# The time steps' weight block second in the stream, and S5's small matmuls issued behind wide blocks of the projection

## The chip, the core and the metric

The kernel runs on one core of one Trainium2 chip. A core has five engines that each run their own program in order and meet only at semaphores: TensorE (PE, matmuls into eight PSUM banks), VectorE (DVE), ScalarE (ACT), GpSimd (POOL) and SyncE (SP, which here only issues DMAs). The metric is the device time of one execution in microseconds, less is better.

## What is computed

Two transformer-like blocks on 512 tokens of width 1024, in float32. The change touches the beginning of the first one, the projection of the normed input and what hangs on it:

```
h = rmsnorm(x, mix_norm_w)
proj = h @ w_in                                  # 1024 x 2828
y_s5 = s5_mixer(proj[:, :256], ...)              # u
y_ssd = ssd_mixer(z = proj[:, 256:1024], xbc = proj[:, 1024:2816], dt_raw = proj[:, 2816:2828], ...)
x = x + concat(y_s5, y_ssd) @ w_out
...
# s5_mixer: 16 groups of 16 channels, 64 complex states each
h_t = a * h_{t-1} + (b u_t);  y = Re(c h) + d u;  y = gelu(y) * sigmoid(gelu(y) @ w_glu)
# ssd_mixer: xbc = silu(causal_conv4(xbc)); dt = softplus(dt_raw + dt_bias); then chunked attention-like sums
```

After it come cross attention over a normed `mem` of 256 rows, a convolutional feed-forward layer, and a second block with two mixers and 16 routed experts.

## The kernel before

Activations lie with channels on partitions (128) and the 512 tokens along the free dimension. Every float32 product is made of three faster ones: a weight is split into a rounded high part `w_hi` and the rest `w_lo`, an activation into `hi` and `lo`, and `pe_fm` sums w_hi·hi, w_hi·lo and w_lo·hi over eight blocks of 128 input channels (lines 474 to 476). One output block of 128 channels is 24 matmuls of 128x512.

Weights come as a stream of slots in the order of the table `STREAM`; `slot_arrays` lays them out in DRAM in the same order. A slot is mostly 256 columns (two output blocks, 48 matmuls); `dt`'s is 128 columns (one block, 24 matmuls). For slot g: SP loads it into one of three raw buffers once DVE has finished slot g-3 (`sp_load`); ACT rounds it to `w_hi` (`act_split`, line 395) when the load is there and PE is through with slot g-2, which used the same of two buffers; DVE subtracts (`dve_split`, line 401); PE waits for DVE, and for the bank of four blocks ago to be emptied (`pe_block_start`). All of this is program order: `act_split_to(k, g)` and `dve_split_to(k, g)` stand where the author put them among the other work of ACT and DVE.

The projection's slots are u, three of xa, dt, xb, za, xc, zb, xd, zc, xe. `IN_TURNS` groups them in turns q = 0 to 4: (x0 x1 x2) (x3 z0) (x4 z1) (x5 z2) (x6), with x0 to x2 in xa and x3 to x6 in xb, xc, xd, xe; three functions walk over it, `pe_w_in`, `act_w_in` and `dve_w_in`. For each x block ACT copies the bank to `pad` and applies the first tap, DVE adds the other three (`dve_taps`), ACT applies silu, in order and one block behind; z blocks are one ACT instruction each.

S5's scan works on 128 chunks of 4 tokens with matrices made on the way:
- `dve_s5_powers` (powers `pw` of the eigenvalues), from which POOL builds the rotation tables `ec` and `es` (`pool_s5_tables`, `s5_double`), by doubling;
- `dve_s5_matrices` makes `bd`; `pe_s5_matrices` turns it by 16 transposes into banks 4 to 7; `act_s5_bt` copies them to `bt`;
- `dve_s5_outputs` makes `cb`; `pe_s5_lags` multiplies it with `bd`; `act_s5_lags` copies the result to `lags`;
- `act_s5_steps` copies `u` to `steps`, 16 copies of 32 partitions;
- for each half h: `pe_s5_in` (steps times bt, into banks 4 and 5), `dve_s5_step` (rotate, scan, rotate back), `pe_s5_out` (lags and cb, into bank 6 + h), `dve_s5_skip`.

Before the change the matrices, the block dt with its four transposes (`pe_dt`), the sum of squares of mem (`pe_norm_sum_all`, line 533) and the lags all stand between the third xa slot and xb, at the end of turn 0. `dve_s5_step` is a generator, issued in pieces between the taps of turns 1 and 2. Behind xe follow the keys (`pe_key`), which need the normed mem (`m_hi`, `m_lo`).

## Time and profile before

| | |
|---|---|
| median of 3 runs | 1543.58 us (1541.92 to 1544.74) |
| the profiled execution | 1542.16 us, span 1541.0 us |
| PE busy | 1420.1 us, 92% of the span |
| PEld (weight loads, beside PE) | 1162.2 us, 75% |
| DVE busy | 978.1 us, 63% |
| ACT busy | 753.3 us, 49% |
| POOL busy | 140.2 us, 9% |
| chain that ended last | PE 67%, DVE 8%, ACT 4%, issue 4%, DMA 1% |
| HBM | mean 150 GB/s over the span |

The page also cuts the span in 40 slices of 38.5 us. Each digit is the busy share in tenths; PEclk is TensorE's granted clock in tenths of full speed. The projection is in slices 1 to 6:

```
PE   7969979899989999999999998999999799999981
PEld 5758868778667888888888887886658688888861
DVE  4847557754325755456546558846545889889876
ACT  5374354544324322122324442245465788887863
PEclk9979999999999999999999999999999899999996
```

A busy PE means matmuls in flight, not matmuls at their peak; a wait is put down to what came last.

### The profile page before, as it was taken

What the parts mean: (1) busy time and instruction counts of PE and PEld (TensorE: products, weight loads), DVE (VectorE), ACT (ScalarE), POOL (GpSimd) and SP (SyncE); (2) the same over time, 40 slices, a digit from 0 to 9 for tenths busy, and PEclk for the clock granted to TensorE, in tenths of its full rate; (3) what the DMA queues carried; (4) which work ended last, traced back from release to release, by engine and by line L of the source; (5) the groups of instructions that cost most, each with busy time, mean ns of one, the idle gap of its engine ahead of it and who ended that gap; (6) DMA issues with size and microseconds to landing.
All of it is one profiled execution on the core that took longest, in us unless ns stands there. A gap on an engine that the chain in (4) does not pass through costs nothing.

```text
span 1541.0 us, 18286 instructions
## 1 busy us (share of the span) xinstructions
PE 1420.1 (92%) x7292; PEld 1162.2 (75%) x7292; DVE 978.1 (63%) x1321; ACT 753.3 (49%) x966; POOL 140.2 (9%) x165
## 2 busy tenths in 40 slices
PE   7969979899989999999999998999999799999981
PEld 5758868778667888888888887886658688888861
DVE  4847557754325755456546558846545889889876
ACT  5374354544324322122324442245465788887863
POOL 1600001100000000000000303200000111111012
PEclk9979999999999999999999999999999899999996
DMA  5112313312103342333123231110006799999975
GB/s 210 68 55 83 137 55 110 110 55 82 56 28 137 126 142 75 111 109 109 66 75 120 87 107 50 60 55 28 28 1 232 267 413 421 412 416 417 408 301 191
DMA packets 39332, 231.62 MB, mean 150 GB/s; under 512 B 4400, under 2 KB 5696, under 8 KB 17104
## 3 DMA queue, kind: packets, MB, share of 16 engines
q1 hardware_dynamic: 30640, 200.09, 34.5%
q0 software_dynamic: 7648, 27.87, 4.8%
q10 hardware_dynamic: 960, 2.49, 0.5%
q8 instruction: 58, 0.95, 0.2%
q14 instruction: 26, 0.21, 0.0%
HBM read 213.66 MB, written 16.78 MB: 150 GB/s over the span
## 4 chain that ended last, share of the span: by engine, by line
PE 67%; DVE 8%; ACT 4%; issue 4%; DMA 1%; POOL 0%; POOLq 0%; DVEq 0%; ACTq 0%
PE bank L474 13%; PE bank L476 12%; PE bank L475 12%; PE bank L3164 5%; PE bank L3166 5%; PE bank L3165 5%; PE bank L620 2%; DVE w_lo L401 1%; PE bank L493 1%; PE bank L494 1%; PE bank L495 1%; PE bank L2393 1%; PE bank L2414 1%; ACT w_hi L395 1%; PE bank L2159 1%
## 5 line engine op out<-in xcount | busy, mean ns | idle before, releaser
L474 PE MATMUL bank<-h_hi,w_hi 128*128 128x512 f32 x952 | 382.1, 401 | 14.1 <-DVE w_lo L401 11.1
L475 PE MATMUL bank<-h_lo,w_hi 128*128 128x512 f32 x952 | 372.2, 391 | 0.0
L476 PE MATMUL bank<-h_hi,w_lo 128*128 128x512 f32 x952 | 371.9, 391 | 0.0
L401 DVE TENSOR_TENSOR w_lo<-w_raw,w_hi 128x2048 fp32r<-128x2048 f32 (+3 forms) x86 | 188.5, 2192 | 116.7 <-ACT w_hi L395 116.1
L474 PEld LDWEIGHTS bank<-h_hi,w_hi 128*128 128x128 f32 x952 | 179.7, 189 | 59.8 <-DVE w_lo L401 14.4
L476 PEld LDWEIGHTS bank<-h_hi,w_lo 128*128 128x128 f32 x952 | 179.5, 189 | 38.2
L475 PEld LDWEIGHTS bank<-h_lo,w_hi 128*128 128x128 f32 x952 | 179.8, 189 | 37.2 <-issue 2.2
L395 ACT ACTIVATE w_hi<-w_raw 128x2048 fp32r<-128x2048 f32 (+3 forms) x87 | 154.8, 1779 | 61.8 <-PE bank L476 61.7
L3349 DVE TENSOR_TENSOR h_lo<-w_raw,h_hi 128x2048 fp32r<-128x2048 f32 x32 | 73.2, 2292 | 10.5 <-ACT h_hi L3250 8.7
L3349 DVE TENSOR_TENSOR lo_b<-raw_b,hi_b 128x2048 fp32r<-128x2048 f32 x32 | 73.2, 2290 | 7.0 <-ACT hi_b L3250 6.8
L474 PE MATMUL bank<-a_hi,w_hi 128*128 128x512 f32 x176 | 68.5, 389 | 0.0
L475 PE MATMUL bank<-a_lo,w_hi 128*128 128x512 f32 x176 | 68.5, 389 | 0.0
L476 PE MATMUL bank<-a_hi,w_lo 128*128 128x512 f32 x176 | 68.5, 389 | 0.0
L1795 ACT ACTIVATE gc<-gc 128x512 f32<-128x512 f32 x22 | 13.9, 632 | 111.4 <-DVE gc L1052 111.4
L3250 ACT ACTIVATE hi_b<-raw_b 128x2048 fp32r<-128x2048 f32 x32 | 61.5, 1921 | 5.7 <-PE bank L3166 5.6
L3250 ACT ACTIVATE h_hi<-w_raw 128x2048 fp32r<-128x2048 f32 x32 | 61.0, 1911 | 0.0
L3164 PE MATMUL bank<-h_hi,hh 128*128 128x512 f32 x128 | 51.2, 400 | 4.1 <-DVE hl L3379 2.6
L3164 PE MATMUL bank<-hi_b,xh 128*128 128x512 f32 x128 | 51.6, 403 | 1.5 <-DVE xl L3356 1.5
L3166 PE MATMUL bank<-lo_b,xh 128*128 128x512 f32 x128 | 50.2, 392 | 0.0
L3166 PE MATMUL bank<-h_lo,hh 128*128 128x512 f32 x128 | 50.1, 391 | 0.0
L3165 PE MATMUL bank<-h_hi,hl 128*128 128x512 f32 x128 | 50.1, 391 | 0.0
L3165 PE MATMUL bank<-hi_b,xl 128*128 128x512 f32 x128 | 49.9, 390 | 0.0
(610 smaller groups left out, 2748.9 us busy)
## 6 DMA issues: line engine op xcount, KB each, us to landing
w_raw<-in_params_dram SPq DMA_DIRECT2D x122, 1024.0 KB, 5.0
raw_b<-in_params_dram SPq DMA_DIRECT2D x51, 1024.0 KB, 8.1
w_raw<-in_params_dram SPq DMA_DIRECT2D x16, 704.0 KB, 4.0
result_rows<-osb POOLq DMA_DIRECT2D x16, 512.0 KB, 8.1
result_rows<-prm POOLq DMA_DIRECT2D x8, 512.0 KB, 3.2
xt<-in_x_t_dram POOLq DMA_DIRECT2D x1, 2048.0 KB, 12.5
scratch_rows<-htm SPq DMA_DIRECT2D x4, 512.0 KB, 2.9
out_dram<-pr SPq DMA_DIRECT2D x4, 512.0 KB, 2.6
```

The lines of the kernel that those rows point to most:

```text
L395: A.activation(k.w_hi[g % SPLIT][:, 0:size], k.raw[:, g % RAW, 0:size], ACT.Copy).then_inc(s.w_hi, 1)
L401: V.tensor_tensor(k.w_lo[g % SPLIT][:, 0:size], k.raw[:, g % RAW, 0:size], k.w_hi[g % SPLIT][:, 0:size].bitcast(F32), ALU.subtract).then_i ...
L474: PE.matmul(ps, wh, hi[:, c, 0:width], start=c == 0, stop=False)
L475: PE.matmul(ps, wh, lo[:, c, 0:width], start=False, stop=False)
L476: m = PE.matmul(ps, wl, hi[:, c, 0:width], start=False, stop=c == parts - 1)
L493: PE.matmul(ps, xh, wh, start=c == 0, stop=False)
L620: return k.nc.tensor.transpose(out, in_, k.ident[0:n, 0:n])
L3164: PE.matmul(o, xh[:, k0 + c, :], wh, start=first and c == 0, stop=False)
L3165: PE.matmul(o, xl[:, k0 + c, :], wh, start=False, stop=False)
L3166: m = PE.matmul(o, xh[:, k0 + c, :], wl, start=False, stop=final and c == 3)
L3250: done(A.activation(w_hi[n], raws[n], ACT.Copy), "w", n, c)
L3349: done(V.tensor_tensor(w_lo[n], raws[n], w_hi[n].bitcast(F32), ALU.subtract), "w", n, c)
```

## The change

`dt` becomes the second slot of the stream, behind u, and its block is multiplied there; its ACT copy goes to `xbc` block 11 (before 13), and its four transposes follow the first xa slot. S5's transposes of bd follow xb (x3); the lags, and then the sum of squares of mem, follow za (z0); `pe_s5_in(0)` follows xc, `pe_s5_in(1)` and `pe_s5_out(0)` follow xd, `pe_s5_out(1)` follows xe. ACT and DVE issue their parts at matching places: ACT's copies of bt behind x3, of lags and the root of mem's norm behind z0; DVE's `dve_s5_outputs` between the split behind x3 and x3's taps, each `dve_s5_step` in one piece at the end of turns 2 and 3. The table `es` moves from `sz` to `xbc` blocks 12 and 13, so ACT's wait for the last rotation moves from z2 to x block 12. The diff:

```diff
--- before.py
+++ after.py
@@ -93,7 +93,7 @@
 
 
 
-STREAM = [("u", 1, "aa"), ("xa", 3, "aa"), ("dt", 1, "a"), ("xb", 1, "aa"), ("za", 1, "aa"), ("xc", 1, "aa"), ("zb", 1, "aa"),
+STREAM = [("u", 1, "aa"), ("dt", 1, "a"), ("xa", 3, "aa"), ("xb", 1, "aa"), ("za", 1, "aa"), ("xc", 1, "aa"), ("zb", 1, "aa"),
           ("xd", 1, "aa"), ("zc", 1, "aa"), ("xe", 1, "aa"),
           ("wk", 4, "aa"), ("wv", 4, "aa"), ("w_out", 4, "vv"), ("wq", 4, "aa"), ("wo", 4, "vv"),
           ("up0", HB, "vv"), ("dn0", DB, "v"), ("up1", HB, "vv"), ("dn1", DB, "v"),
@@ -148,7 +148,7 @@
 def slot_arrays(a):
 
     xbc, z = columns(a["w_in"][0], 1024, 1792), columns(a["w_in"][0], 256, 768)
-    s = columns(a["w_in"][0], 0, 256) + xbc[:3] + columns(a["w_in"][0], 2828 - P, P, P)
+    s = columns(a["w_in"][0], 0, 256) + columns(a["w_in"][0], 2828 - P, P, P) + xbc[:3]
     s += [xbc[3], z[0], xbc[4], z[1], xbc[5], z[2], xbc[6]]
     for n in ("xa_wk", "xa_wv", "w_out", "xa_wq", "xa_wo"):
         s += columns(a[n][0], 0, D)
@@ -243,7 +243,7 @@
         self.pad = m("pad", [P, 2, T + 3])
         self.tt = self.sz[:, 0:4, :].rearrange("p a t -> p (a t)").rearrange("p (i j l) -> p i j l", i=2, j=8)
         self.rm = self.rs[:, 0:MEM]
-        self.ec, self.es = m("ec", [P, TILES, CHUNKS]), self.sz[:, 4:6, :].rearrange("p a (t c) -> p (a t) c", c=CHUNKS)
+        self.ec, self.es = m("ec", [P, TILES, CHUNKS]), self.xbc[:, 12:14, :].rearrange("p a (t c) -> p (a t) c", c=CHUNKS)
         x = Memory(nc, x_at, h_at)
         self.bu, self.gg = x("bu", [P, 2, TILES // 2, CHUNKS]), x("gg", [P, 2, TILES // 2, CHUNKS])
         self.steps, self.lags = x("steps", [P, TILES, CHUNKS]), x("lags", [P, TILES, P])
@@ -976,17 +976,14 @@
     v(V.tensor_tensor(t0, im, es, ALU.mult))
     v(V.tensor_tensor(g1, im, ec, ALU.mult))
     v(V.tensor_tensor(t1, re, es, ALU.mult))
-    yield
     v.own()
     v(V.tensor_tensor(g0, g0, t0, ALU.add))
     v(V.tensor_tensor(g1, g1, t1, ALU.subtract))
-    yield
     v.own()
     for t in range(4):
         mag = k.mag[:, STEPS - 1, 4 * h + t:4 * h + t + 1].broadcast_to([P, CHUNKS])
         for part, g in enumerate((g0, g1)):
             v(V.tensor_tensor_scan(bu[part][:, t, :], mag, g[:, t, :], 0.0, ALU.mult, ALU.add))
-    yield
     v.own()
     V.tensor_tensor(g0, bu[0], ec, ALU.mult).then_inc(s.s5_rot, 1)
     V.scalar_tensor_tensor(g1, bu[1], -1.0, es, ALU.mult, ALU.mult).then_inc(s.s5_rot, 1)
@@ -1082,23 +1079,28 @@
     for c in range(DB):
         for j in range(2):
             pe_fm(k, "u", 0, j, k.hi, k.lo, "mix", first=c, stop=c + 1)
+    pe_fm(k, "dt", 0, 0, k.hi, k.lo, cols=P)
     for q, turn in enumerate(IN_TURNS):
         for x, (part, n) in enumerate(turn):
             stage, slot = in_slot(part, n)
             for j in range(2):
                 pe_fm(k, stage, slot, j, k.hi, k.lo)
-            if x == 0 and q in (2, 3):
-                pe_s5_out(k, q - 2)
-            if x == 0 and q in (1, 2):
-                pe_s5_in(k, q - 1)
-        if q == 0:
-            PE.wait_ge(s.n_rs, 1)
-            pe_s5_matrices(k)
-            pe_fm(k, "dt", 0, 0, k.hi, k.lo, cols=P)
-            PE.wait_ge(s.s5_bt, 4)
-            pe_norm_sum_all(k, "mem", k.msq, MEM, 7)
-            pe_dt(k)
-            pe_s5_lags(k)
+            if (part, n) == ("x", 0):
+                PE.wait_ge(s.n_rs, 1)
+                pe_dt(k)
+            elif (part, n) == ("x", 3):
+                pe_s5_matrices(k)
+            elif (part, n) == ("z", 0):
+                PE.wait_ge(s.s5_bt, 4)
+                pe_s5_lags(k)
+                pe_norm_sum_all(k, "mem", k.msq, MEM, 7)
+            elif (part, n) == ("x", 4):
+                pe_s5_in(k, 0)
+            elif (part, n) == ("x", 5):
+                pe_s5_in(k, 1)
+                pe_s5_out(k, 0)
+            elif (part, n) == ("x", 6):
+                pe_s5_out(k, 1)
     for b in range(2):
         pe_key(k, b)
     pe_ssd_sums(k)
@@ -1112,7 +1114,7 @@
     PE, s = k.nc.tensor, k.s
     PE.wait_ge(s.evac_a, EMPTIED[BLOCK0["dt"]][1])
     for t in range(TT):
-        m = pe_turn(k, k.bank[4][:, t * P:t * P + P], k.xbc[:, XBC_B - 1, t * P:t * P + P])
+        m = pe_turn(k, k.bank[4][:, t * P:t * P + P], k.xbc[:, 11, t * P:t * P + P])
     m.then_inc(s.dt_turn, 1)
 
 
@@ -1130,8 +1132,10 @@
         act_norm_hi(k, "mix", k.sq0, k.hi, 0, b, T)
     act_split_to(k, 1)
     act_s5_angle(k)
+    act_split_to(k, SLOT0["xa"])
     for j in range(2):
         act_empty(k, BLOCK0["u"] + j, k.u[:, j, :])
+    act_empty(k, BLOCK0["dt"], k.xbc[:, 11, :])
 
     def silu(blk):
         A.wait_ge(s.conv, blk + 1)
@@ -1149,6 +1153,8 @@
                         A.wait_ge(s.pads_zero, 1)
                     if blk >= 2:
                         A.wait_ge(s.conv, blk - 1)
+                    if blk == 12:
+                        A.wait_ge(s.s5_rot, 8)
                     act_empty(k, i, k.pad[:, blk % 2, 3:T + 3])
                     A.wait_ge(s.evac_a, EMPTIED[i][1])
                     A.activation(k.xbc[:, blk, :], k.pad[:, blk % 2, 0:T], ACT.Identity, bias=k.col("ssd_cb", blk),
@@ -1158,8 +1164,6 @@
                 else:
                     if n == 0 and j == 0:
                         A.wait_ge(s.s5_tab, 2)
-                    elif n == 2 and j == 0:
-                        A.wait_ge(s.s5_rot, 8)
                     act_empty(k, i, k.sz[:, 2 * n + j, :], ACT.Silu)
             if part == "x" and n == 6:
                 silu(XBC_B - 1)
@@ -1173,12 +1177,11 @@
                 A.wait_ge(s.mem, 16)
                 for b in range(DB):
                     act_square(k, "mem", k.mt, k.msq, b, MEM)
-        if q == 0:
-            act_s5_bt(k)
-            act_split_to(k, SLOT0["dt"] + 1)
-            act_empty(k, BLOCK0["dt"], k.xbc[:, XBC_B - 1, :])
+            if (part, n) == ("x", 3):
+                act_s5_bt(k)
+        if q == 1:
+            act_s5_lags(k)
             act_norm_root(k, "mem", k.rm, k.bank[7][:, 0:MEM], D)
-            act_s5_lags(k)
             act_ssd_steps(k)
 
 
@@ -1189,13 +1192,15 @@
     dve_norm_split(k, "mix", k.xt, k.col("mix_norm", 0, DB), k.sq0, k.rs, k.hi, k.lo, 0, DB, T, slot=0)
     dve_split_to(k, 1)
     dve_s5_powers(k)
+    dve_split_to(k, SLOT0["xa"])
     for q, turn in enumerate(IN_TURNS):
-        step = dve_s5_step(k, q - 1) if q in (1, 2) else iter(())
         for n_, (part, n) in enumerate(turn):
             stage, slot = in_slot(part, n)
             dve_split_to(k, SLOT0[stage] + slot + 1)
-            if q == 0 and n_ == 1:
+            if (part, n) == ("x", 1):
                 dve_s5_matrices(k)
+            elif (part, n) == ("x", 3):
+                dve_s5_outputs(k)
             if part == "x":
                 for j in range(2):
                     blk = 2 * n + j
@@ -1204,19 +1209,16 @@
             if part == "x" and n == 6:
                 dve_norm_split(k, "mem", k.mt, k.col("mem_norm", 0, DB), k.msq, k.rm, k.mhi, k.mlo, 0, DB, MEM)
                 dve_split_to(k, SLOT0["wk"] + 1)
-            for _ in range(3):
-                next(step, None)
-        for _ in step:
-            pass
-        if q == 0:
-            dve_split_to(k, SLOT0["dt"] + 1)
-            dve_s5_outputs(k)
-            V.wait_ge(s.dt_turn, 1)
-            tm = k.bank[4][:, :].rearrange("p (t c) -> p t c", t=TT)[:, :, P - SSD_H:P]
-            V.tensor_copy(k.dtr[:, :, :], tm).then_inc(s.dt_out, 1)
+            if (part, n) == ("x", 0):
+                V.wait_ge(s.dt_turn, 1)
+                tm = k.bank[4][:, :].rearrange("p (t c) -> p t c", t=TT)[:, :, P - SSD_H:P]
+                V.tensor_copy(k.dtr[:, :, :], tm).then_inc(s.dt_out, 1)
+        if q == 1:
             dve_ssd_steps(k)
-        if q in (2, 3):
-            dve_s5_skip(k, q - 2)
+        elif q in (2, 3):
+            dve_s5_step(k, q - 2)
+        if q in (3, 4):
+            dve_s5_skip(k, q - 3)
```

What this does to the order of instructions, at three places. First ACT, behind its second split; w_hi_53 and w_hi_54 are the two buffers of the high part, u, xbc and pad what is copied from PSUM (+ is the kernel after):

```order
-L395 ACTIVATE w_hi_54<-w_raw 128x2048
+L395 ACTIVATE w_hi_54<-w_raw 128x1024
 L685 ACT_TABLE_LOAD
 L685 ACTIVATE s5sc<-s5sc 128x8
 L686 ACTIVATE s5sc<-s5sc 128x8
+L395 ACTIVATE w_hi_53<-w_raw 128x2048
 L504 ACTIVATE u<-bank 128x512 x2
-L395 ACTIVATE w_hi_53<-w_raw 128x2048
```

The second split is dt's half slot, and xa's first split stands ahead of the copies of u instead of behind them.

DVE, behind the powers pw; w_lo_55 and w_lo_56 are the two buffers of the low part. Before:

```order
L731 TENSOR_TENSOR pw<-s5sc 128x8
L401 TENSOR_TENSOR w_lo_55<-w_raw,w_hi_53 128x2048
L1052 SCALAR_TENSOR_TENSOR xbc<-pad,prm,xbc 128x512 x6
L401 TENSOR_TENSOR w_lo_56<-w_raw,w_hi_54 128x2048
L745 TENSOR_TENSOR lam<-pw,mag 128x2x8 x3
L746 TENSOR_TENSOR s5t<-pw 128x16
L747 TENSOR_TENSOR s5t<-pw 128x16
L749 TENSOR_TENSOR lam<-s5t 128x8
```

and after:

```order
L731 TENSOR_TENSOR pw<-s5sc 128x8
L401 TENSOR_TENSOR w_lo_55<-w_raw,w_hi_53 128x2048
L401 TENSOR_TENSOR w_lo_56<-w_raw,w_hi_54 128x2048
L1049 SCALAR_TENSOR_TENSOR xbc<-pad,prm,xbc 128x512 x6
L1215 COPY dtr<-bank 128x48
L401 TENSOR_TENSOR w_lo_55<-w_raw,w_hi_53 128x2048
L745 TENSOR_TENSOR lam<-pw,mag 128x2x8 x3
L746 TENSOR_TENSOR s5t<-pw 128x16
```

The split behind the powers was that of xa's second slot and is now that of its first, which PE takes next; another whole split follows ahead of the first taps, and the copy of the time steps (dtr) stands ahead of the split in front of the matrices (lam).

PE, around the small matmuls (bd transposed, msq summed, xbc transposed for dt, cb times bd). Before:

```order
L476 MATMUL bank3<-h_hi_58,w_lo1_56 128x512
L620 MATMUL bank4<-ident_62,bd_89 128x128 x4
L620 MATMUL bank5<-ident_62,bd_89 128x128 x4
L620 MATMUL bank6<-ident_62,bd_89 128x128 x4
L620 MATMUL bank7<-ident_62,bd_89 128x128 x4
...
L476 MATMUL bank0<-h_hi_58,w_lo0_55 128x512
L533 MATMUL bank7<-msq_104,ones_63 128x256 x8
L620 MATMUL bank4<-ident_62,xbc_68 128x128 x4
L882 MATMUL bank5<-cb_78,bd_89 32x128 x8
L882 MATMUL bank6<-cb_78,bd_89 32x128 x8
L474 MATMUL bank1<-h_hi_58,w_hi1_54 128x512
```

and after:

```order
L476 MATMUL bank2<-h_hi_58,w_lo1_56 128x512
L620 MATMUL bank4<-ident_62,bd_89 128x128 x4
L620 MATMUL bank5<-ident_62,bd_89 128x128 x4
L620 MATMUL bank6<-ident_62,bd_89 128x128 x4
L620 MATMUL bank7<-ident_62,bd_89 128x128 x4
L474 MATMUL bank3<-h_hi_58,w_hi0_53 128x512
...
L476 MATMUL bank0<-h_hi_58,w_lo0_55 128x512
L882 MATMUL bank5<-cb_78,bd_89 32x128 x8
L882 MATMUL bank6<-cb_78,bd_89 32x128 x8
L533 MATMUL bank7<-msq_104,ones_63 128x256 x8
L474 MATMUL bank1<-h_hi_58,w_hi1_54 128x512
```

The 16 transposes have 48 wide matmuls of xb ahead of them and za's behind; lags and sum have changed places and stand behind za; dt's block (bank0 above) and its transposes are gone from here.

## Rows read from the trace of the kernel before

**Rows 1.** Instructions in order of time on PE: start, length (us), engine, line, what, [idle before].

```profile
37.25 0.50 PE L474 MATMUL bank<-h_hi,w_hi 128*128 128x512 f32 x1 [0.16 <-DVE w_lo L401]
...
70.19 0.39 PE L476 MATMUL bank<-h_hi,w_lo 128*128 128x512 f32 x1
...
73.48 3.05 PE L620 MATMUL bank<-ident,bd 128*128 128x128 f32 x16 [2.90 <-DVE bd L799]
...
84.01 0.80 PE L474 MATMUL bank<-h_hi,w_hi 128*128 128x512 f32 x1 [7.49 <-DVE w_lo L401]
...
94.62 5.17 PE L533 MATMUL bank<-msq,ones 128*128 128x256 f32 x15 [3.12 <-ACT bt L838]
...
104.84 5.34 PE L882 MATMUL bank<-cb,bd 128*32 128x128 f32 x32 [4.40 <-DVE cb L826]
...
110.11 0.50 PE L474 MATMUL bank<-h_hi,w_hi 128*128 128x512 f32 x1
```

**Rows 2.** Stretches: length, busy PE, PEld, DVE, ACT, POOL, then PEclk, DMA.

```profile
37.20:110.10 72.90, 54.91 (x236) 44.40 (x236) 47.80 (x115) 39.74 (x60) 24.91 (x42) 0.86 0.19 66
110.10:199.70 89.60, 89.59 (x689) 74.90 (x688) 52.27 (x74) 36.50 (x46) 2.95 (x4) 1.00 0.31 106
73.40:76.50 3.10, 3.02 (x16) 2.68 (x16) 2.99 (x5) 0.78 (x2) 0.00 (x0) 0.62 0.00 0
84.00:91.50 7.50, 7.49 (x24) 5.72 (x24) 4.42 (x6) 6.75 (x12) 0.00 (x0) 0.75 0.40 140
94.60:99.80 5.20, 5.18 (x16) 4.28 (x17) 3.26 (x3) 3.67 (x3) 0.00 (x0) 0.67 0.00 0
104.80:110.10 5.30, 5.26 (x32) 4.49 (x32) 0.60 (x3) 1.50 (x4) 0.00 (x0) 0.68 0.01 3
173.10:177.70 4.60, 4.60 (x162) 4.34 (x161) 2.82 (x4) 3.73 (x4) 0.00 (x0) 1.00 0.02 4
```

**Rows 3.** Order of time on ACT, around the first copies to steps.

```profile
75.72 0.63 ACT L1138 ACTIVATE xbc<-xbc 128x512 f32<-128x512 f32 x1 [14.85 <-DVE xbc L1052]
...
76.26 5.36 ACT L850 ACTIVATE steps<-u 32x256 f32<-32x256 f32 x8
...
81.64 1.06 ACT L395 ACTIVATE w_hi<-w_raw 128x1024 fp32r<-128x1024 f32 x1
```

**Rows 4.** Order of time on DVE, S5's matrices and the split behind them.

```profile
59.23 2.04 DVE L745 TENSOR_TENSOR lam<-pw,mag 128x16 f32<-128x16 f32 x3
...
64.87 0.15 DVE L753 TENSOR_TENSOR s5sc<-s5sc 128x8 f32<-128x8 f32 x1
...
73.36 4.56 DVE L1052 SCALAR_TENSOR_TENSOR xbc<-pad,prm,xbc 128x512 f32<-128x512 f32 x6
...
82.73 1.23 DVE L401 TENSOR_TENSOR w_lo<-w_raw,w_hi 128x1024 fp32r<-128x1024 f32 x1 [4.80 <-ACT w_hi L395]
```

**Rows 5.** Order of time on POOL, the last instruction of the tables.

```profile
63.62 1.29 POOL L899 TENSOR_TENSOR sz<-sz 128x512 f32<-128x512 f32 x1
```

**Rows 6.** Order of time on ACT, behind the second split.

```profile
34.89 1.28 ACT L685 ACT_TABLE_LOAD   x1
...
36.30 0.19 ACT L686 ACTIVATE s5sc<-s5sc 128x8 f32<-128x8 f32 x1
```

**Rows 7.** Order of time on DVE, the powers and the split behind them.

```profile
37.11 0.16 DVE L719 TENSOR_TENSOR s5sc<-s5sc 128x8 f32<-128x8 f32 x1
...
42.96 2.29 DVE L401 TENSOR_TENSOR w_lo<-w_raw,w_hi 128x2048 fp32r<-128x2048 f32 x1
```

**Rows 8.** Order of time on ACT, the norm of mem to the time steps.

```profile
101.83 0.42 ACT L542 ACTIVATE rs<-rs 128x256 f32<-128x256 f32 x1
...
108.53 3.58 ACT L862 ACTIVATE lags<-bank 32x128 f32<-32x128 f32 x8 [6.28 <-PE bank L882]
...
115.67 1.90 ACT L395 ACTIVATE w_hi<-w_raw 128x2048 fp32r<-128x2048 f32 x1
```

**Rows 9.** Order of time on PE, the first matmul of the keys.

```profile
205.17 0.55 PE L474 MATMUL bank<-m_hi,w_hi 128*128 128x256 f32 x1 [5.48 <-DVE m_lo L554]
```

## The prediction

> **What bounds the kernel now.** I read the page first: PE is busy 92% of the span, DVE 63%, ACT 49%, and the chain that ended last is mostly matmuls. So the end is set by TensorE's program order plus the places where TensorE stands still, and a change that moves nothing but order can only win or lose such places. Next, the busy time by stretch [rows 2]. The change touches the input projection. Its second part, 110.1 to 199.7 us, is full: 89.59 of 89.60 us busy at granted clock 1.00, so the other engines are always early enough there. The first part, 37.2 to 110.1 us, is not: 54.91 of 72.90 us busy, clock 0.86. Then the instructions of PE in order of time [rows 1], for the idle time in the brackets. Three 256-column slots (u is done by 37.1) run through without a pause until 70.6. Behind them PE waits 2.90 us for DVE's bd, does 16 transposes, waits 7.49 us for the dt slot's low part, multiplies dt, waits 3.12 us for ACT's copies of bt, sums the squares of mem, waits 4.40 us for DVE's cb, and does the lags. That is 17.9 us of waiting. It is a row of small steps, each with an answer from DVE or ACT, and no wide block of matmuls stands between them to cover the answer.
>
> The clock makes it dearer. In the four small pieces it was granted at 0.62, 0.75, 0.67 and 0.68 [rows 2], that is partly at 1.2 and partly at 2.4 GHz, after waits of 2.9 to 7.5 us; in the full stretches it is 1.00. At 1.00 the pieces would take 1.9, 5.6, 3.5 and 3.6 us for 3.1, 7.5, 5.2 and 5.3: 6.5 us lost.
>
> **What the change does to these pieces.** The dt slot (24 matmuls) goes to second place, so its split stands ahead of xa's. The transposes of bd follow xb instead of the third xa slot; the lags and the sum of mem follow za; s5's inputs follow xc and xd, its outputs follow xd and xe. TensorE's instructions are the same ones; nothing is added. If every answer comes during the 11 us of a wide slot, the ledger is: 17.9 us of waits gone, 6.5 us of slow clock gone, and a third term: the second output block (4.6 us at clock 1.00) [rows 2] now stands behind xe. There PE waits 5.48 us for the normed mem in any case [rows 9], a chain of ACT and DVE that starts at xe's end, so the 4.6 us are hidden and some 0.9 us of that wait stays. Credit: 17.9 + 6.5 + 4.6 = 29.0 us.
>
> **What is late instead: xa's first split.** Two debits stand against that, and I work them out from times of DVE and ACT. The slot unit first: 144 matmuls from 37.25 to 70.19 [rows 1], so 0.23 us each, 11.0 us a wide slot, 5.5 us for dt. PE leaves u at 37.1 and dt at 42.6. xa's first slot uses u's buffers of the high and low part, so ACT splits it only after u, at 37.1 to 39.0, and DVE takes it after its powers (they stand ahead of it in its program). The powers take 42.96 - 37.11 = 5.85 us [rows 7]. They begin when ACT's table load and two sines are over: 36.49 - 34.89 = 1.6 us behind its split [rows 6], and this split is now of half a slot, 1.06 us for 1.90 [rows 3, 8], so it ends at 34.05. Powers then 35.65 to 41.5, split 2.29 us [rows 7], done 43.8. PE starts xa at 43.85: a wait of 1.2 us, and everything in xa comes 6.6 us later than now. A wait as short as this costs no clock, I take; in the worst case it costs what followed the 2.9 us wait, 1.2 us.
>
> **What is late instead: xb's split.** This is the large debit. The 7.49 us wait was not the transposes' fault. DVE starts S5's matrices at 59.23 behind the third xa split, reaches the taps at 73.36 [rows 4], and ACT, in order, holds its silu for those taps 14.85 us; then come 5.36 us of copies to steps, and only then the next split [rows 3]. The change leaves these where they are. The split behind them is now xb's, a whole slot, and dt's short slot with its transposes no longer stands there. Chain: the matrices start at 59.23 + 6.6 = 65.8. Of their 14.1 us, the nine small instructions up to 64.87 took 5.6 us, three of them 2.04 us, where the like instruction after it took 0.15 us [rows 4]. POOL's tables end at 64.9 [rows 5]; they start from the powers, 1.5 us earlier now (35.65 for 37.11), so they end near 63.5 and are clear of the matrices. I price the nine at 1.3 us, hence 1.3 + 8.5 = 9.8 us: done 75.6. Taps to silu 2.36, silu to steps 0.54, steps to split 5.38 [rows 3, 4]: 83.9. Split to matmul was 84.01 - 81.64 = 2.37 for half a slot; a whole one adds 0.84 on ACT and 1.06 on DVE (2.29 for 1.23) [rows 4, 7]: 4.3, so xb starts at 88.1. PE comes out of xa at 70.6 + 6.6 and 0.5 for dt's four transposes, 77.7. It waits 10.4 us. Behind it, as behind the 7.49 us wait, the slow clock: 7.5 - 5.6 = 1.9 us.
>
> The Trainium skill, SBUF — State Buffer, section Who interferes with whom, says that a DVE instruction with two SBUF inputs and a GpSimd instruction that reads SBUF exclude each other for a whole instruction, each in turn. By that rule the 4.3 us of relief are real, as soon as POOL is through; without it, the nine might be slow by themselves (broadcast operands), and the relief would be nothing. This case's rows lean to the rule: the fast 0.15 us begins at 64.87, the moment at which POOL ends.
>
> **Is anything late behind xb?** From 88.1: xb with slow clock to 101.0, transposes 1.9, za to 113.9, lags 3.6, mem's sum 3.5, so xc from 121.0 to 132.0. The tightest is zb's split, since ACT does the root of mem's norm, then the time steps, ahead of it: root done 102.25 - 99.8 = 2.4 us behind the sum, then 115.67 - 112.1 = 3.6 [rows 8], splits 1.9 + 2.3: 131.3. PE needs it after xc and s5's first input, at 1.7 us ((89.6 - 7 x 11.0 - 2 x 4.6) / 2) [rows 2]: 133.7. Slack 2.4 us. bt's copies follow the taps of block 6, which stand behind cb (about 6 us of DVE): some 111 against 113.9. DVE's scans (9 us) now run in one piece, 138 to 147, against 155 when PE asks; x block 12 waits for the second scans, done some 12 us before. SP loads in the new order, each slot's load is let go three slots ahead, as now. POOL's reload of xt (2 MB) waits for the second output block and moves with it, far ahead of its use. All at nothing; each would show as a wait of PE.
>
> **Sum.** Credit 29.0; debits 1.2 + 10.4 + 1.9 = 13.5; and 0.1 for rounding: 15.4 us. The profiled execution took 1542.16 us (span 1541.0, 1.2 around it): 1526.8. The median of the runs is 1.4 higher, so 1528.2. Ends for the uncertain terms: relief 0 instead of 4.3; small wait's clock 1.2; lags, sum and transposes as long as today (4.6 in all) if the clock dips again; the other way, no slow clock behind the wait, 1.9, and xa's third split earlier by what POOL is out of its way, some 0.7. One by one and added up: 1525.6 to 1538.3.
>
> **Rivals.** A, the matrices stay slow: the nine instructions take 5.6 us wherever they stand, or POOL is slower in its new company and runs into them. Then xb starts at 92.4, 11.1 us are gained: 1532.5. For it: POOL has to share DVE with a split and taps meanwhile, as today. Against: the 64.87 boundary. 15%.
> B, a second wait behind xb: zb's slack of 2.4 us is used up, and ACT's queue, with lags, roots and time steps in one row, passes its lateness on to DVE's splits, each of which starts the next. One missed slot costs up to a wide slot, 11 us, once more: 1539, up to no gain. For it: ACT and DVE are in order and share one chain. Against: the stretch from 110 us is full today under nearly this load. 6%.
> C, the other side: the clock. The new 10.4 us wait is the longest of the stage. If TensorE stayed at 1.2 GHz not for part of a slot but through xb, the transposes, za, the lags and mem's sum (31 us of work), it would lose 31 us instead of 1.9, and the kernel would be 13.7 us slower: 1557.3. It decides from 17 us of work at the low level on. Against: after 7.49 us of waiting the clock was back within the 24 matmuls of dt (0.75 on the mean). 3%. The Trainium skill, TensorE: Matmul & The Clock Gate, section Seeing it yourself, tells of a clock seen stuck low over a long stretch; no row here shows it.
> D, that the change does nothing: the waits come back somewhere else in full, as the keys need mem's norm anyway. The chain there starts at xe's end, and xe's end is what moves. 3%.
>
> **Chances.** My forecast 73%, A 15%, B 6%, C 3%, D 3%. The range of 1524 to 1536 holds the forecast's and A's ends with the 1.4 us between runs; outside are the most of B, C and D. This kernel's measurement tells 0.2%, 3.1 us, from no change. Faster by more: 0.93; within: 0.03; slower: 0.04.
>
> **What would show it.** Right: PE's idle time between 37 and 185 us is two waits, about 1.2 us ahead of xa and about 10 ahead of xb, the second released by DVE's split of xb, with ACT's silu still held for DVE's taps; clock 1.00 in lags and mem's sum; the small instructions of the matrices at 0.15 us; the keys start near 189.8 instead of 205.17, after 1 us of waiting; and behind it the same trace, shifted. Wrong: a wait above 13 us at xb (A), any wait at zb, xd or zc (B), a clock below 1.00 behind za (C). Should the keys start at 190 and the end move by less, the loss is in later stages, which I take as shifted as a whole.

## The result: 1.0% faster, where the forecast was 1.0%

The changed kernel took 1527.51 us (median of four, 1525.25 to 1528.59), the kernel before beside it 1543.28 (1541.92 to 1544.74): a ratio of 0.9896, with a 95% interval of 0.9879 to 0.9913. The forecast was 1528.2 us. A second set of five runs of the same changed kernel, told below, gave 1527.16. Two executions of 3667 us, one of the kernel before in a later set and one of the kernel with the second output block in its old place, are left out of all medians here.

The profiled execution took 1525.25 us, with a span of 1524.1 for the 1541.0 of before. It is the fastest of the nine executions of this kernel in the two sets; the second trace, told below, is of the slowest, 1531.33 us. TensorE is busy 1413.3 us (93%), DVE 975.3, ACT 752.5, GpSimd 140.6. The first view to read is again TensorE's order of time. Columns as in [rows 1]: start, length, engine, line, what, and in brackets the idle time before it.

```profile
43.80 0.50 PE L474 MATMUL bank<-h_hi,w_hi 128*128 128x512 f32 x1 [1.70 <-DVE w_lo L401]
...
87.02 0.80 PE L474 MATMUL bank<-h_hi,w_hi 128*128 128x512 f32 x1 [9.79 <-DVE w_lo L401]
...
99.57 1.91 PE L620 MATMUL bank<-ident,bd 128*128 128x128 f32 x16
...
112.30 3.68 PE L882 MATMUL bank<-cb,bd 128*32 128x128 f32 x32
115.91 3.72 PE L533 MATMUL bank<-msq,ones 128*128 128x256 f32 x16
...
130.38 1.95 PE L934 MATMUL bank<-steps,bt 128*128 128x128 f32 x16
...
187.87 0.36 PE L474 MATMUL bank<-m_hi,w_hi 128*128 128x256 f32 x1 [0.99 <-DVE m_lo L554]
...
190.78 0.39 PE L474 MATMUL bank<-m_hi,w_hi 128*128 128x256 f32 x1 [0.93 <-DVE m_lo L554]
...
208.44 1.98 PE L1023 MATMUL bank<-u,wglu 128*128 128x512 f32 x4 [0.99 <-ACT u L1003]
```

Against [rows 1]: the waits ahead of the transposes (2.90), of the sum of mem (3.12) and of the lags (4.40) are gone; these three pieces carry no bracket at all. The wait ahead of a slot's low part is still there, 7.49 us before and 9.79 now, but a wide slot, xb's, stands behind it. The other new wait is ahead of xa. Its bracket shows 1.70 us, but a bracket only measures from the last matmul that was recorded, and in other executions of this kernel and its variants the same gap is shown as 0.23 to 1.74 with xa starting at 43.3 to 44.1 in all eleven; so the start is the number to read. The keys begin at 187.87 for 205.17 [rows 9].

The stretches of the same trace (length, busy PE, PEld, DVE, ACT, POOL, then granted clock, DMA):

```profile
36.00:111.50 75.50, 64.02 (x284) 52.47 (x284) 51.40 (x118) 42.86 (x61) 24.49 (x42) 0.93 0.25 84
87.00:100.00 13.00, 12.98 (x52) 10.66 (x53) 7.01 (x8) 10.60 (x15) 0.00 (x0) 0.87 0.23 81
99.50:101.50 2.00, 2.00 (x18) 1.93 (x17) 1.97 (x5) 1.42 (x2) 0.00 (x0) 1.00 0.49 78
112.30:115.90 3.60, 3.60 (x33) 3.41 (x32) 2.60 (x3) 2.46 (x7) 0.00 (x0) 1.00 0.25 34
115.90:119.60 3.70, 3.70 (x18) 3.27 (x18) 0.00 (x0) 3.19 (x6) 0.00 (x0) 1.00 0.60 250
110.00:186.00 76.00, 76.00 (x627) 64.67 (x629) 47.58 (x72) 37.87 (x51) 0.00 (x0) 1.00 0.25 84
```

These answer to [rows 2]. The transposes, the lags and the sum of mem had 0.62, 0.68 and 0.67; each now follows a wide slot and runs at 1.00. The lags take 3.6 us for 5.3. What is left of the slow clock sits in xb, 0.87, behind the long wait. From 110 to 186 us TensorE is busy without a gap, so nothing is late behind xb.

The chain that sets xb's start, on ACT, answering to [rows 3]:

```profile
76.82 0.63 ACT L1142 ACTIVATE xbc<-xbc 128x512 f32<-128x512 f32 x1 [8.92 <-DVE xbc L1049]
77.36 5.35 ACT L850 ACTIVATE steps<-u 32x256 f32<-32x256 f32 x8
82.73 1.91 ACT L395 ACTIVATE w_hi<-w_raw 128x2048 fp32r<-128x2048 f32 x1
```

and on DVE, answering to [rows 4] and [rows 7]:

```profile
41.45 2.29 DVE L401 TENSOR_TENSOR w_lo<-w_raw,w_hi 128x2048 fp32r<-128x2048 f32 x1
...
65.06 0.33 DVE L745 TENSOR_TENSOR lam<-pw,mag 128x16 f32<-128x16 f32 x3
...
65.96 0.16 DVE L753 TENSOR_TENSOR s5sc<-s5sc 128x8 f32<-128x8 f32 x1
...
74.46 4.56 DVE L1049 SCALAR_TENSOR_TENSOR xbc<-pad,prm,xbc 128x512 f32<-128x512 f32 x6
84.67 2.29 DVE L401 TENSOR_TENSOR w_lo<-w_raw,w_hi 128x2048 fp32r<-128x2048 f32 x1 [5.65 <-ACT w_hi L395]
...
127.23 2.29 DVE L401 TENSOR_TENSOR w_lo<-w_raw,w_hi 128x2048 fp32r<-128x2048 f32 x1 [1.52 <-ACT w_hi L395]
```

The eight small instructions of S5's matrices ahead of L753 run from 65.06 to 65.96, 0.90 us for 5.64 before; three of them are 0.33 us for 2.04. (The prediction and the expectations count them as nine; the traces have eight up to L753's start.) ACT's silu still waits for DVE's taps, 8.92 us for 14.85. Then silu, copies to steps, split, split, xb: the same chain as before, link for link. GpSimd's last table instruction, answering to [rows 5]:

```profile
61.70 1.28 POOL L899 TENSOR_TENSOR xbc<-xbc,sz 128x512 f32<-128x512 f32 x1
```

It ends at 62.98, ahead of the matrices at 65.06. Before, it ended at 64.91, and they had begun at 59.23.

### The profile page after: what moved, and what is told of

The parts are those of the page before. It is cut to its first block, busy times and chain, and to the rows that moved or that the text cites. A ratio compares the mean times of both kernels' runs of the same rounds, so it can differ in the third digit from the quotient of the medians.

```text
span 1524.1 us, 18285 instructions
## 1 busy us (share of the span) xinstructions
PE 1413.3 (93%) x7292; PEld 1157.5 (76%) x7292; DVE 975.3 (64%) x1321; ACT 752.5 (49%) x966; POOL 140.6 (9%) x165
## 4 chain that ended last, share of the span: by engine, by line
PE 67%; DVE 8%; ACT 4%; issue 4%; DMA 1%; POOL 0%; POOLq 0%; DVEq 0%; ACTq 0%
PE bank L474 13%; PE bank L476 12%; PE bank L475 12%; PE bank L3166 5%; PE bank L3168 5%; PE bank L3167 5%; PE bank L620 2%; DVE w_lo L401 2%; PE bank L493 1%; PE bank L495 1%; PE bank L494 1%; PE bank L2416 1%; PE bank L2395 1%; ACT w_hi L395 1%; PE bank L2161 1%
## 5 line engine op out<-in xcount | busy, mean ns | idle before, releaser
L474 PE MATMUL bank<-h_hi,w_hi 128*128 128x512 f32 x952 | 381.2, 400 | 17.9 <-DVE w_lo L401 14.9
L401 DVE TENSOR_TENSOR w_lo<-w_raw,w_hi 128x2048 fp32r<-128x2048 f32 (+2 forms) x86 | 187.8, 2184 | 107.1 <-ACT w_hi L395 106.5
L395 ACT ACTIVATE w_hi<-w_raw 128x2048 fp32r<-128x2048 f32 (+2 forms) x87 | 154.8, 1780 | 62.9 <-PE bank L476 62.9
L1797 ACT ACTIVATE gc<-gc 128x512 f32<-128x512 f32 x22 | 13.9, 632 | 111.4 <-DVE gc L1049 111.4
```

Source lines behind the costliest of these rows:

```text
L395: A.activation(k.w_hi[g % SPLIT][:, 0:size], k.raw[:, g % RAW, 0:size], ACT.Copy).then_inc(s.w_hi, 1)
L401: V.tensor_tensor(k.w_lo[g % SPLIT][:, 0:size], k.raw[:, g % RAW, 0:size], k.w_hi[g % SPLIT][:, 0:size].bitcast(F32), ALU.subtract).then_i ...
L474: PE.matmul(ps, wh, hi[:, c, 0:width], start=c == 0, stop=False)
```

## Experiments

The theory that is tested is the prediction's ledger: each wait saved or added is worth its length and the slow clock behind it; the wait ahead of xb is DVE's and ACT's chain behind S5's matrices. Each experiment has its own rival, in its expectation. All diffs are against the changed kernel, save for the first one. "The changed kernel" is put at 1527.3 us, the median of its nine runs in two sets. The gated block is S5's last step, u times wglu, and its start on TensorE (L1023, after ACT's 0.99 us) is the mark by which the traces are compared behind the keys.

### The dt block alone

The kernel before, with nothing but the dt slot in second place: its splits ahead of xa's, TensorE's dt matmuls and transposes behind the third x slot. All S5 work stays where it was.

```diff
-STREAM = [("u", 1, "aa"), ("xa", 3, "aa"), ("dt", 1, "a"), ...
+STREAM = [("u", 1, "aa"), ("dt", 1, "a"), ("xa", 3, "aa"), ...
...
             pe_s5_matrices(k)
-            pe_fm(k, "dt", 0, 0, k.hi, k.lo, cols=P)
```

> The kernel before with dt's slot second in the stream, its block behind u and its transposes behind the first xa slot; the transposes of bd, mem's sum and the lags stay between xa and xb, the outputs where they were. Ledger theory (the gain is waits taken away plus clock, part by part): xa ends at 77.1, the transposes follow at once, then PE waits for bt until about 97 (ACT does both groups of copies to steps first), sum and lags 9 us, xb starts near 106 for 110.1 before. About 4 us faster than before: 1539.5. Rival (dt's place carries the gain, the rest moves what was hidden): all of the change's 15.8 us, 1527.5.

Measured: 1538.01 us, ratio to the kernel before 0.997 (0.9956 to 0.9983). TensorE in order of time:

```profile
76.77 1.91 PE L620 MATMUL bank<-ident,bd 128*128 128x128 f32 x16
97.33 6.72 PE L533 MATMUL bank<-msq,ones 128*128 128x256 f32 x16 [18.65 <-ACT bt L838]
```

A wait of 18.65 us stands behind the transposes, in front of the sum of mem, because bt's copies on ACT stand behind the taps, steps and a split. The waits of 2.90, 7.49, 3.12 and 4.40 have become this one, and behind it the sum of mem runs at the low clock (6.72 us for the 3.72 in the changed kernel). The keys start at 202.67, after 5.48 us as before. The ledger's 1539.5 stands against the rival's 1527.5: by the medians dt's place alone is worth 4 us of the 16 (2.5 us at the keys' start and 2.8 at the gated block in this one trace), and the rest comes from the S5 pieces moving behind wide slots.

### The early splits

xb's and za's splits are taken out of the queue behind the taps: ACT splits xb ahead of the silus of blocks 2 and later, DVE directly behind S5's matrices; the steps, bt's copies and za's split move up in the same way.

```diff
+                    if blk == 3:
+                        act_split_to(k, SLOT0["xb"])
+                        act_s5_steps(k, (0, 1))
+                    elif blk == 5:
+                        act_split_to(k, SLOT0["za"])
+                    elif blk == 7:
+                        act_s5_bt(k)
...
                 dve_s5_matrices(k)
+                dve_split_to(k, SLOT0["xb"])
...
+                    if blk == 5:
+                        dve_split_to(k, SLOT0["za"])
```

> The changed kernel with xb's split taken out from behind the silu that waits for DVE: ACT splits xb behind x block 3's first tap and does the first half of the copies to steps there, DVE takes it behind the matrices, ahead of the taps; za's split likewise behind x block 5's first tap; ACT's copies of bt ahead of the silu of block 6. Ledger theory: xb's low part is there at 76.7, xa ends at 77.1, so the 9.8 us wait and 1.5 us of slow clock go and no other wait takes their place: 11.3 us faster than the changed kernel, 1516.2. Rival (ACT and DVE are one full chain, and the wait only moves on to za or zb): under 3 us faster, 1525 or more.

Measured: 1513.74 us, ratio 0.9817 (0.9797 to 0.9836).

```profile
43.86 0.50 PE L474 MATMUL bank<-h_hi,w_hi 128*128 128x512 f32 x1 [0.37 <-DVE w_lo L401]
...
88.02 1.91 PE L620 MATMUL bank<-ident,bd 128*128 128x128 f32 x16
...
176.35 0.36 PE L474 MATMUL bank<-m_hi,w_hi 128*128 128x256 f32 x1 [1.00 <-DVE m_lo L554]
...
197.34 1.98 PE L1023 MATMUL bank<-u,wglu 128*128 128x512 f32 x4 [0.99 <-ACT u L1003]
```

No bracket between 43.86 and 176.35: the wait ahead of xb is gone, and no other took its place. The transposes start 11.55 us earlier (88.02 for 99.57), which is the wait of 9.79 and the slow clock of xb behind it. That is the ledger's price for this wait. It reaches the end: 11.1 us at the gated block (197.34 for 208.44), and 13.6 us by this median, 10.4 by that of a second set of runs, told below.

### Does GpSimd slow the small instructions?

The theory of the 4.3 us term: the eight small instructions are slow only while GpSimd's tables run. Test: xa's first split ahead of DVE's powers, which removes the wait ahead of xa but starts the tables 6.5 us later, so that they run into the matrices again.

```diff
-    dve_s5_powers(k)
     dve_split_to(k, SLOT0["xa"])
+    dve_s5_powers(k)
```

> The changed kernel with DVE's split of xa's first slot ahead of the powers, not behind. PE's 1.7 us wait ahead of xa goes. If DVE's small instructions were slow because of POOL: the powers, and with them POOL's tables, come 5.4 us later, the tables end near 68 and lie over the nine small instructions of the matrices, which take about 5.6 us for 0.9: xb starts 2.6 us or more later, 1530. Rival (POOL plays no part): 1.7 us faster, 1525.8.

Measured: 1532.54 us, ratio 0.9936 (0.9917 to 0.9956), so slower than the changed kernel by 5 us. On DVE:

```profile
64.25 2.04 DVE L745 TENSOR_TENSOR lam<-pw,mag 128x16 f32<-128x16 f32 x3
...
69.88 0.15 DVE L753 TENSOR_TENSOR s5sc<-s5sc 128x8 f32<-128x8 f32 x1
```

on GpSimd:

```profile
62.13 3.09 POOL L894 TENSOR_TENSOR sz<-xbc,pw 128x512 f32<-128x512 f32 x1
...
68.65 1.27 POOL L899 TENSOR_TENSOR xbc<-xbc,sz 128x512 f32<-128x512 f32 x1
```

and on TensorE:

```profile
90.95 0.80 PE L474 MATMUL bank<-h_hi,w_hi 128*128 128x512 f32 x1 [14.54 <-DVE w_lo L401]
```

The same three instructions take 2.04 us again, and they are fast from 69.88 on; GpSimd's last table instruction ends at 69.92. Before, the pair of times was 64.87 and 64.91. In both kernels the boundary follows GpSimd and not the place in the program. GpSimd pays too: one 128x512 instruction that takes 1.05 us in the changed kernel took 3.09 here, beside DVE's split, as it did in the kernel before. xb starts at 90.95 for 87.02. I had expected 3 us of loss and measured 5: behind the wait of 14.54 us xb takes 13.5 us for 12.6, and the keys' part is 0.5 us longer.

The ends show how: GpSimd's instructions in this trace end at 66.26, 67.29, 68.68 and 69.92 us, and DVE's long instructions at 66.29, 67.31, 68.71 and 69.96, each 0.02 to 0.04 us behind one of GpSimd's; the two between them take 0.16 and 0.17 us. The Trainium skill (SBUF — State Buffer, section Who interferes with whom) says that a DVE instruction with two SBUF inputs contends with a GpSimd instruction that reads SBUF, for ports that only one of them holds at a time. The trace agrees: 5.63 us here against 0.90 in the changed kernel for the same eight instructions.

### The second output block in its old place

```diff
-            elif (part, n) == ("x", 6):
+            elif (part, n) == ("z", 2):
                 pe_s5_out(k, 1)
```

> The changed kernel with the second output block behind zc, ahead of xe, and not behind xe. Ledger theory: its 4.6 us come back onto the path, since the chain of mem's norm starts at xe's end; PE's wait ahead of the keys grows from 1.0 to 5.5 us; 4.5 us slower than the changed kernel, 1532.0. Rival (the keys' wait is set elsewhere): no difference, 1527.5.

Measured: 1528.16 us (median of five), ratio 0.9907 (0.9889 to 0.9926): 0.9 us slower than the changed kernel, where 4.5 were expected. The intervals overlap, so the medians alone would not show that it is slower at all.

```profile
193.06 0.55 PE L474 MATMUL bank<-m_hi,w_hi 128*128 128x256 f32 x1 [5.47 <-DVE m_lo L554]
...
211.66 1.98 PE L1023 MATMUL bank<-u,wglu 128*128 128x512 f32 x4 [0.99 <-ACT u L1003]
```

The wait ahead of the keys is back at 5.47 us, as expected, and the keys start 4.4 to 5.2 us later than in the two traces of the changed kernel (187.87 and 188.63). But the gated block starts only 2.2 to 3.2 us later: from the keys' start to it, this kernel takes 18.60 us, and the changed one 20.57. So part of the hidden block's worth is lost between keys and gated block. In the changed kernel's trace, DVE there:

```profile
189.11 0.85 DVE L562 SCALAR_TENSOR_TENSOR msq<-mt,prm,rs 128x256 f32<-128x256 f32 x1
189.88 0.85 DVE L554 TENSOR_TENSOR m_lo<-msq,m_hi 128x256 fp32r<-128x256 f32 x1
```

and GpSimd:

```profile
188.98 1.48 POOL L604 TENSOR_SCALAR_AFFINE_SELECT afm<-afm 128x512 fp32r<-128x512 f32 x2
```

GpSimd waits for the second output block before it reloads xt and builds afm. Both moved with the block, and the two selects now meet DVE's norm of mem: two instructions take 0.85 us each for 0.48 and 0.42. (The memset just ahead of the selects, 188.37 to 188.91 us, slows nothing: DVE's two instructions beside it take 0.48 and 0.41.) TensorE waits a second time (0.93 us at 190.78 above), and behind that wait its clock dips:

```profile
193.50:196.50 3.00, 3.00 (x18) 3.00 (x17) 0.00 (x1) 2.99 (x3) 0.00 (x0) 0.56 0.63 254
```

### GpSimd's work behind mem's norm

```diff
+    G.wait_ge(s.m_mul, DB)
     k.g(G.memset(exact, -1.0))
...
-    G.wait_ge(s.m_mul, DB)
```

> The changed kernel, with GpSimd's memset and two affine selects of afm held until DVE has normed the last block of mem. Theory (GpSimd's selects slow two of DVE's instructions of mem's norm from 0.48 and 0.42 to 0.85 us, the keys wait a second time for m_lo, and their matmuls run at a lower clock behind that wait): DVE's L562 and L554 all at 0.4 to 0.5 us, one wait of 1.0 us ahead of the keys and no second one, keys to gated block 18.6 us for 20.6 to 20.9, so glu starts about 206.5. Time 2 us under the changed kernel's 1527.3: 1525.3. Rival 1 (the selects only stand where DVE would be slow anyway): keys to glu stays 20.6 to 20.9 and the time 1527.3. Rival 2 (the pieces behind it take the gain back, since the clock after each later wait varies from run to run by as much): glu 2 us earlier, time 1527.3.

Measured: 1524.78 us, ratio 0.9886 (0.9868 to 0.9903). TensorE:

```profile
187.80 0.36 PE L474 MATMUL bank<-m_hi,w_hi 128*128 128x256 f32 x1 [1.00 <-DVE m_lo L554]
...
206.40 1.98 PE L1023 MATMUL bank<-u,wglu 128*128 128x512 f32 x4 [0.99 <-ACT u L1003]
```

and DVE:

```profile
189.03 0.48 DVE L562 SCALAR_TENSOR_TENSOR msq<-mt,prm,rs 128x256 f32<-128x256 f32 x1
189.43 0.42 DVE L554 TENSOR_TENSOR m_lo<-msq,m_hi 128x256 fp32r<-128x256 f32 x1
```

Keys to gated block is 18.60 us again, with one wait; the two instructions are back at 0.48 and 0.42. The first theory holds in the trace to a tenth: 2.0 us earlier at the gated block. The medians say 2.5 us, which agrees but would not prove it, as the intervals overlap.

Of the 2.0 us, the two instructions explain 0.8. The rest is about the price of the clock, 0.56 in the stretch above and 1.00 in this kernel: from 193.36 to 195.93 us twelve matmuls of the changed kernel start 0.21 us apart, where they start 0.12 apart here, an estimate of 1.1 us. A low clock does not cost the same everywhere: with the output block in its old place the keys begin at 0.50 (193.0 to 196.0 us), are back at 1.00 from 198.8, and their stretch still takes 9.90 us, as here at 1.00 throughout (9.91). There the dip falls on the first keys, which have to wait for DVE's m_lo at either clock; in the changed kernel it comes when DVE is done and TensorE sets the pace. No run parts the wait from the clock behind it.

### TensorE kept at work in the wait

80 transposes of the identity into a bank that nobody reads, ahead of xb.

```diff
+            if (part, n) == ("x", 3):
+                pe_keep_on(k, 6, 80)
             for j in range(2):
                 pe_fm(k, stage, slot, j, k.hi, k.lo)
```

> The changed kernel with 80 more transposes of the identity into bank 6, which nobody reads, in PE's 9.8 us wait ahead of xb (80 x 0.119 = 9.5 us); they compute nothing. If the wait costs its length and, behind it, the slow clock: xb takes 11.0 us for 12.55, 1.5 us faster than the changed kernel. Rival (the clock behind the wait is not tied to PE standing still): no difference.

Measured: 1523.45 us, ratio 0.9888 (0.9868 to 0.9908).

```profile
76.86 8.90 PE L620 MATMUL bank<-ident 128*128 128x128 f32 x80
87.09 0.50 PE L474 MATMUL bank<-h_hi,w_hi 128*128 128x512 f32 x1 [1.33 <-DVE w_lo L401]
...
98.12 1.91 PE L620 MATMUL bank<-ident,bd 128*128 128x128 f32 x16
```

xb starts at the same time (87.09 for 87.02) and takes 11.03 us for 12.55. So against the first trace the slow clock behind the wait costs 1.5 us, and the gated block starts at 206.92, again 1.5 us earlier. By the medians it is 3.8 us. The two ratios to the kernel before, 0.9896 and 0.9888, are not told apart by their intervals, so the 1.5 us of the trace is the figure to keep.

### The transposes of bd in the wait

The same place, but with useful work: the 16 transposes go ahead of xb instead of behind it.

```diff
+            if (part, n) == ("x", 3):
+                pe_s5_matrices(k)
             for j in range(2):
                 pe_fm(k, stage, slot, j, k.hi, k.lo)
...
-            elif (part, n) == ("x", 3):
-                pe_s5_matrices(k)
```

> The changed kernel with the 16 transposes of bd in the wait ahead of xb and not behind xb; bd is there at 74.4, xa ends at 77.1. Ledger theory: a small piece put into a wait costs nothing, behind a wide block it costs its length: 1.9 us faster than the changed kernel, the slow clock in xb as before. Rival (what stands behind a wide block is free): no difference.

Measured: 1524.76 us, ratio 0.9881 (0.986 to 0.9902).

```profile
77.10 1.91 PE L620 MATMUL bank<-ident,bd 128*128 128x128 f32 x16
87.09 0.79 PE L474 MATMUL bank<-h_hi,w_hi 128*128 128x512 f32 x1 [8.08 <-DVE w_lo L401]
```

The transposes fit into the wait, which is 8.08 us instead of 9.79, and xb starts at the same time. The lags start at 110.78 and the keys at 186.36, both 1.5 us earlier than in the first trace of the changed kernel and 2.3 earlier than in the second, whose xb was slower; that brackets the 1.9 us expected. The gated block starts at 206.11, 2.3 us earlier than in the first trace, as the keys' stretch was shorter too. So behind xb the transposes cost their length, and in the wait they cost nothing. Ahead of xb in the kernel before they had a wait of 2.90 us in front of them and ran at 0.62; neither is there now, as bd is done before xa ends.

### The changed kernel once more

> The changed kernel once more, unaltered, beside the others on one chip, as what they are compared with: 1526 to 1528 by every theory.

Measured: 1527.16 us, ratio 0.9898 (0.988 to 0.9916).

```profile
87.07 0.80 PE L474 MATMUL bank<-h_hi,w_hi 128*128 128x512 f32 x1 [9.79 <-DVE w_lo L401]
...
100.29 1.91 PE L620 MATMUL bank<-ident,bd 128*128 128x128 f32 x16
```

xa starts at 43.86 and xb at 87.07, behind the same 9.79 us, but the transposes at 100.29 instead of 99.57. So xb took 13.2 us here and 12.55 in the first trace, by the same program: the slow clock behind the same wait cost 2.3 and 1.7 us, over the 10.9 us of a slot at full clock (xc, from the end of mem's sum at 119.5 to the first input at 130.4).

### The best version, twice

The early splits together with GpSimd's work behind mem's norm (both diffs above).

> The kernel with the early splits (e4) and POOL's memset and two selects on afm held back until DVE has normed mem. In the changed kernel these fall on DVE's norm of mem, one pair of its instructions takes 0.85 us each for 0.48 and 0.42. If POOL is the reason: 0.8 us faster than e4, some 1513. Rival: no difference from e4, 1513.7.

Measured: 1512.93 us, ratio 0.9802 (0.9782 to 0.9821). This is the fastest so far, but only 0.8 us ahead of the early splits' 1513.74, and not the 2.6 us that its own trace shows at the gated block (194.73 for 197.34). At 418 us the two traces stand at the same transposes again (418.49 and 418.74). To see whether that is the program or chance, both ran again side by side.

> The early splits once more, beside the next kernel on one chip. By both theories the median lies at 1513 to 1515 us, keys at 176.3 and glu at 197.3 us in the trace. If the clock behind the later waits is a matter of chance, the time at which the time-step scans' last matmuls run (275 to 287 us, granted clock 0.89 in the first run of this kernel, 0.77 in that of the next) has another clock this time.

> The early splits with GpSimd's afm work behind mem's norm, once more, beside the kernel without the latter on one chip. If the 2.6 us that it is ahead at the gated block reach the end, its median is 2 to 2.6 us under the other's: 1511 to 1512. If the slow clock behind the later waits takes them back, the medians are equal within 1 us. In the trace: keys at 176.1, glu at 194.7, and the piece from 272 to 286 us at a granted clock of 0.77 again if the arrival time decides it, at another clock if chance does.

Measured, early splits: 1516.86 us, ratio 0.9836 (0.982 to 0.9853). With GpSimd's work later: 1512.43, ratio 0.9819 (0.9801 to 0.9837). One piece of the program shows a part of what the trace of the later version had lost. It begins behind a wait of 3.2 us on DVE, with the last products of the scan over chunks (the piece that the expectations name by its 275 to 287 us), and ends where the next norm is multiplied. Stretches as above: length, busy PE, PEld, DVE, ACT, POOL, granted clock, DMA. Early splits, the keys' stretch and this piece in the first set, then the piece in the second:

```profile
176.30:188.60 12.30, 11.16 (x64) 10.53 (x64) 8.48 (x15) 7.94 (x12) 2.69 (x5) 0.72 0.53 175
...
275.00:287.10 12.10, 10.84 (x63) 8.51 (x63) 7.52 (x12) 6.41 (x8) 0.00 (x0) 0.89 0.00 1
```
```profile
274.20:285.80 11.60, 9.45 (x62) 7.17 (x62) 7.40 (x12) 6.41 (x8) 0.00 (x0) 1.00 0.01 1
```

With GpSimd's work later, first and second:

```profile
176.10:186.00 9.90, 9.26 (x64) 7.91 (x64) 6.43 (x14) 7.96 (x12) 2.61 (x5) 1.00 0.63 214
...
272.30:285.60 13.30, 11.99 (x62) 9.53 (x62) 7.54 (x13) 6.41 (x8) 0.00 (x0) 0.77 0.00 1
```
```profile
272.10:283.70 11.60, 9.46 (x62) 7.17 (x62) 7.41 (x12) 6.41 (x8) 0.00 (x0) 1.00 0.01 1
```

In the keys' stretch the later version is ahead: 9.9 us at a clock of 1.00 for 12.3 at 0.72 (in the second set 9.9 for 11.4 at 0.85). In the other piece, the busy time of DVE and ACT is the same in all four (7.4 to 7.5 and 6.4 us); the granted clock is 0.89, 1.00, 0.77 and 1.00, and the piece lasts 12.1, 11.6, 13.3 and 11.6 us. One program has had both the slowest and the fastest of them. So the clock behind such a wait is not fixed by the program, and this piece alone moves an execution by 1.7 us. In the first set it took 1.1 us of the lead. Most of the rest went in the last 14 us ahead of the transposes at 418: from 404.80 they took 13.9 us at a clock of 0.88, and 12.3 at 1.00 in the early splits' trace. Over both sets of ten runs the version with GpSimd's work later has a median of 1512.7 us and the early splits 1514.8: 2.1 us, beside the 2.6 and 2.1 us that the two pairs of traces show at the gated block (194.73 for 197.34, 194.48 for 196.60). The runs of the two kernels overlap.

## Why the prediction was right

The median, 1527.5, lies 0.7 us under the forecast. Step by step, with the times at which TensorE starts each piece:

```
                       forecast   first trace   second trace
xa                       43.85       43.80         43.86
xb                       88.1        87.02         87.07
transposes of bd        101.0        99.57        100.29
lags                    113.9       112.30        113.05
keys                    189.8       187.87        188.63
gated block (glu)       208.7       208.44        209.51
```

(208.7 is the start in the trace of before, the row below, less the 15.4 us of the forecast.)

```profile
224.09 1.98 PE L1026 MATMUL bank<-u,wglu 128*128 128x512 f32 x4 [0.99 <-ACT u L1006]
```

**The credits.** The four waits of 17.9 us in all went, as the ledger counts them, and so did the slow clock in the pieces behind them: right, with clocks of 1.00 for 0.62 to 0.68 [rows 2].

**The wait ahead of xa.** Right: 43.80 for 43.85, and no dip of the clock behind it (1.00 from 43.8 to 77.3 us).

**The wait ahead of xb.** The mechanism was right link by link, and the early splits confirm it by removing the wait. The start was 1.1 us early against the forecast: 0.7 because S5's matrices began at 65.06 and not 65.8, the third xa split being out of GpSimd's way (it had been named as an end, not taken), and 0.4 because the small instructions, eight and not nine, took 0.90 us and not 1.3. The wait itself is 9.8 us for 10.4: less by only 0.6, since TensorE came out of xa at 87.02 - 9.79 = 77.23 and not at 77.7: dt's four transposes, put at 0.5 us, hardly show.

**The slow clock behind it.** Forecast 1.9; measured 1.7 and 2.3 in two traces, or 1.5 and 2.2 against the kernel that filled the wait. Right within what one program shows of itself.

**Nothing late behind xb.** Right: 76.00 of 76.00 us busy from 110. zb's split is done at 127.23 + 2.29 = 129.5 and needed when xc's slot and then s5's first input are over, at 130.4 + 1.9 = 132.3: slack 2.8 for the 2.4 of the forecast.

**The mis-sized term.** "So the 4.6 us are hidden and some 0.9 us of that wait stays": the wait was right (0.99), the price was not. What the forecast put under "all at nothing", GpSimd's reload of xt and what follows it moving with the second output block, has an answer: its selects meet DVE's norm of mem. Count from TensorE's last work ahead of the keys (their start less the wait) to the gated block: 211.66 - (193.06 - 5.47) = 24.1 us with the block in its old place, 208.44 - (187.87 - 0.99) = 21.6 in the changed kernel, 206.40 - (187.80 - 1.00) = 19.6 with GpSimd's work later. So the move brings 2.5 us, and 4.5 only where the selects are out of the way. This error of 2 us and the keys' start, 1.9 us earlier than forecast, cancel: the gated block begins 0.3 us from its forecast. So a part of the closeness is luck: the number was closer than its terms were.

**The rivals.** A, the small instructions stay slow: false here, and the experiment with the split ahead of the powers shows that it would have come true with tables that start later; xb then started at 90.95. B, a second wait behind xb: false, no bracket. C, the clock stays low: false, 0.87 in xb and 1.00 from there on. The Trainium skill (TensorE: Matmul & The Clock Gate, section Seeing it yourself) tells of a clock stuck low; no run here shows it. D, the change is given back: false for the most of it; what is given back is the 2 us by GpSimd.

**What stays open.** The span fell by 16.9 us, and TensorE was only 15.65 us ahead at the gated block. The same comparison gives 14.6 and 10.8 us for the second trace (1530.2 us of span). Some of the second is a transfer: near the end TensorE waits 2.44 us for the rows `xg` (at 1488 us) where it waited 1.10 us in the trace of before, and the 4.2 us behind it ran at a clock of 0.63; together that is 2.6 of the 3.8 us between 14.6 and 10.8. Why that transfer came later is open. Other late pieces differ in clock from one execution to the next, as shown above for two of them; that this explains the rest was not shown.

## What to carry to other kernels

Count the small dependent steps of a stage and put each behind a wide block of TensorE's work: what is saved is the wait and, behind it, the slow clock, which here was a third as much again. Then look for the one in-order engine that now feeds the wide blocks: the split that the next wide block needs must not stand behind another stage's elementwise work on the same queue; the early splits gave 12.6 us (medians of ten runs and of nine of the changed kernel, 1514.75 and 1527.31), beside the 15.8 of the whole change. And when a block moves, follow every engine that waits for it, down to idle ones: GpSimd's release moved with the output block, and its selects fell on DVE's critical instructions.
